# First dilated attention: dilated units and cross-attention units in alternation

## The reference, cut to what matters

```python
for g, (window, dilation) in enumerate(((128, 1), (512, 4), (2048, 16))):      # 4 heads of 128 each
    o, lse = dilated_window_attention(q[:, :, sl], k[:, :, sl], v[:, :, sl], window, dilation)
# softmax over the three groups' lse weighs their outputs; 512 columns come out

p = softmax(einsum('bshd,bmhd->bhsm', q, k) * XA_HEAD_DIM ** -0.5)             # 4 heads of 64, 256 memory tokens
o = einsum('bhsm,bmhd->bshd', p, v)                                            # 256 columns, beside the 512
```

## Time and profile before

| | us |
|---|---|
| median of 3 runs (lowest to highest) | 2457.7 (2454.57 to 2458.89) |
| the profiled execution, as timed | 2457.92 |
| its span, first to last instruction | 2456.1 |
| in it, `da0`, from its first weight load on PE to its last output copy | 1315.97 to 1379.38 |

### The profile page before, as it was taken

How to read it: one execution, slowest core, us unless ns; L and a number is a source line. 1 busy time by engine, 2 the same in 40 slices (tenths; PEclk the granted TensorE clock), 3 DMA queues, 4 the chain that set the end, 5 groups by cost and what they waited for, 6 DMA issues and landing times. The chain is left out here.

```text
span 2456.1 us, 32385 instructions
## 1 busy us (share of the span) xinstructions
PE 2395.0 (98%) x11700; PEld 2030.8 (83%) x11700; DVE 1722.0 (70%) x2910; ACT 1030.7 (42%) x2126; POOL 200.8 (8%) x269
## 2 busy tenths in 40 slices
PE   7999999999999999999999999999999999999998
PEld 7998877888888888878888889887788888888877
DVE  4522564479899989896653563563679998998996
ACT  6433553344444444446334433433344444443443
POOL 2010012000000000003212021121100000000000
PEclk9999999999999999999999999999999999999999
DMA  4230122222222248743102111212632222227863
GB/s 148 83 104 20 40 84 61 86 72 84 79 94 86 77 139 305 268 133 129 52 18 83 35 35 45 60 35 75 210 96 78 86 78 78 95 81 258 292 191 126
DMA packets 206517, 257.72 MB, mean 105 GB/s; under 512 B 38376, under 2 KB 141784, under 8 KB 206360
## 3 DMA queue, kind: packets, MB, share of 16 engines
q1 hardware_dynamic: 202200, 255.65, 31.7%
q10 hardware_dynamic: 4160, 0.02, 0.1%
HBM read 206.54 MB, written 49.09 MB: 104 GB/s over the span
## 5 line engine op out<-in xcount | busy, mean ns | idle before, releaser
L52 PE MATMUL psum<-f_T_lo 128*128 128x512 f32 x616 | 241.6, 392 | 1.4 <-DVE f_T_lo L683 0.8
L53 PE MATMUL psum<-f_T_lo 128*128 128x512 f32 x616 | 239.8, 389 | 0.0
L54 PE MATMUL psum<-f_T_lo 128*128 128x512 f32 x616 | 239.8, 389 | 0.0
L52 PE MATMUL psum<-w_hi,hT_hi 128*128 128x512 f32 x576 | 229.3, 398 | 3.9 <-DVE w_lo L1469 2.2
L54 PE MATMUL psum<-w_hi,hT_lo 128*128 128x512 f32 x576 | 226.4, 393 | 0.0
L53 PE MATMUL psum<-w_lo,hT_hi 128*128 128x512 f32 x576 | 226.1, 393 | 0.0
L52 PEld LDWEIGHTS psum<-w_hi,hT_hi 128*128 128x128 f32 x576 | 124.8, 217 | 22.0 <-issue 3.6
L52 PEld LDWEIGHTS psum<-f_T_lo 128*128 128x128 f32 x616 | 115.6, 188 | 30.5 <-DVE f_T_lo L683 7.1
L54 PEld LDWEIGHTS psum<-w_hi,hT_lo 128*128 128x128 f32 x576 | 125.0, 217 | 18.0
L53 PEld LDWEIGHTS psum<-w_lo,hT_hi 128*128 128x128 f32 x576 | 125.1, 217 | 16.7
L52 PE MATMUL psum<-hT_hi,f_up_hi 128*128 128x512 f32 x352 | 137.4, 390 | 0.4 <-DVE f_up_lo L622 0.4
(11 more groups left out here) (434 smaller groups left out, 6014.6 us busy)
## 6 DMA issues: line engine op xcount, KB each, us to landing
raw<-in_ffn_w_up_dram SPq DMA_DIRECT2D x88, 512.0 KB, 4.7
activations<-f_act SPq DMA_DIRECT2D x44, 512.0 KB, 2.6
w_raw<-in_b_w_in_dram SPq DMA_DIRECT2D x18, 1024.0 KB, 6.2
f_up_pieces<-activations SPq DMA_DIRECT2D x30, 512.0 KB, 4.4
f_up_pieces<-in_ffn_w_down_dram SPq DMA_DIRECT2D x22, 512.0 KB, 4.9
x_between<-XY SPq DMA_DIRECT2D x16, 512.0 KB, 5.1
XY<-x_between SPq DMA_DIRECT2D x16, 512.0 KB, 6.6
w_raw<-in_a_w_in_dram SPq DMA_DIRECT2D x8, 768.0 KB, 5.8
```

The costliest lines, as they stand in the source:

```text
L52: nc.tensor.matmul(out, lhs_hi, rhs_hi, start=start, stop=False)
L53: nc.tensor.matmul(out, lhs_hi, rhs_lo, start=False, stop=False)
L54: return nc.tensor.matmul(out, lhs_lo, rhs_hi, start=False, stop=stop)
```

## The change

The list of `da0` is put in another order. The first two staged tiles (8 units) stay in front. Behind them, 24 pairs follow, each of one staged unit and one cross unit, until the staged units are used up; the last 8 cross units end the list. Each unit gets a kind, "staged" or "rest", and a number among those of its kind. What was found by a unit's place in the list (the column of its row sum, its tile in the store's count, the wait for the loaded keys) is found by kind and number. SP waits for the place of a tile's fourth head before it stores the tile, and for that of the last staged unit before it stores the row sums.

```diff
+    kinds = [u[7] for u in units]
+    number = [kinds[0:i].count(kinds[i]) for i in range(U)]
+    place = [i for i in range(U) if kinds[i] == "staged"]
+    first_rest = kinds.index("rest") if "rest" in kinds else U
...
         def neg_top(u):
-            return group_top[:, u:u + 1] if u < staged else rest_top[:, u - staged:u - staged + 1]
+            return (group_top if kinds[u] == "staged" else rest_top)[:, number[u]:number[u] + 1]
...
-                    if loads and i == staged:
+                    if loads and i == first_rest:
                         pe.wait_ge(loaded, 16 * len(loads))
...
-                    if u >= staged:
+                    if kinds[u] == "rest":
                         nc.vector.reciprocal(total(u), total(u)).then_inc(inverted, 1)
...
-                    if u < staged:
-                        if u % 4 == 0 and stage.before(u // 4):
-                            act.wait_ge(stage.stored[u // 4 % 2], stage.before(u // 4))
+                    if kinds[u] == "staged":
+                        t = number[u] // 4
+                        if number[u] % 4 == 0 and stage.before(t):
+                            act.wait_ge(stage.stored[t % 2], stage.before(t))
                         nc.scalar.activation(out, src, ACT.Copy).then_inc(out_done, 1)
                     else:
-                        act.wait_ge(inverted, u - staged + 1)
+                        act.wait_ge(inverted, number[u] + 1)
...
             for t in range(TT):
-                sp.wait_ge(out_done, 4 * t + 4)
+                sp.wait_ge(out_done, place[4 * t + 3] + 1)
                 stage.store(sp, t)
...
             if U > staged:
-                sp.wait_ge(expd, staged)
+                sp.wait_ge(expd, place[-1] + 1)
                 stage.store_sums(sp)
...
-                        units += xa_units(lambda h, t: XQ[:, t, h // 2 * P:(h // 2 + 1) * P], keys, vals, D_DIL)
+                        cross = xa_units(lambda h, t: XQ[:, t, h // 2 * P:(h // 2 + 1) * P], keys, vals, D_DIL)
+
+                        both = [u for pair in zip(units[2 * DIL_HEADS:], cross) for u in pair]
+                        units = units[0:2 * DIL_HEADS] + both + cross[len(both) // 2:]
```

## The result

The changed kernel takes 2461.93 us in the median (20 runs, 2457.1 to 2464.57), the kernel before in runs beside it 2458.52 (20 runs, 2453.3 to 2462.76). The ratio is 1.0014, with a 95% interval of 1.0008 to 1.0020: 3.4 us slower, a small loss that is real. 2461.9 was forecast.

The account below looks back on a forecast made before the run. PE, busy 98% of the span, was taken as the bound, so only its waits and clock in `da0` could change. Pairs 41.58, cross steps, end and low clock made 54.3 us against 50.31: 2457.92 + 4.0 = 2461.9, range 2456 to 2466.

Parts of the forecast that it names:

- The pair: In da0's alternation, one staged plus one cross step would take 1.98 us against 1.755 before, 0.225 lost on each.
- the last piece: End of the cross units' loop on PE, product's weight load to next scores: 0.39 us, or 0.45 with PE full.
- The chain: Cross units' two-step loop through PE and DVE: scores, reduction, copy, product, next cross scores; 1.95 to 2.01 us.
- The waits named beforehand: PE's weight load of the cross product would wait about 0.3 us for DVE's copy, 20-odd times; staged products no more.
- The hole: PE's idle stretch early in da0, while ACT waits for staging tile 0's store; would shrink from 3.7 to about 2.4 us.
- low piece: Stretch of about 3.4 us behind PE's idle stretch in da0 with PE at half clock, costing 1.36 us after the change.
- the third rival: PE's clock stays up after the shorter idle stretch in da0: 1.36 us comes off, +2.6, 2460.5 us; chance 0.17.
- The sum: From unit 14's scores to da0's end: 54.3 us after against 50.31 before, a difference of +4.0 us.
- PE alone: Rival: PE's own work sets each staged-and-cross pair in da0 at 1.66 us; -2.7, 2455.2 us; chance 0.08.
- the plain sum: Rival: a staged-and-cross pair in da0 costs its parts, 1.755 us; -0.7, 2457.2 us; chance 0.07.
- The clock in the alternation: Rival: PE's clock falls during da0's pairs, half of 41.6 us at 1.2 GHz; +8 more, 2470 us; chance 0.06.
- DVE's order: Rival: in da0 a late staged copy delays the cross reduction by up to 0.29 us a pair; 2468 us; chance 0.06.

Follow-up runs that it names:

- the lengthened loop: Changed kernel plus a second DVE copy of 128 columns of each cross unit's transposed probabilities, ahead of the real copy: 2467.48 us, one run.

## Why the prediction was right

**The pair.** This was the step that carried the forecast, and it held: 2.01 us where 1.95 to 2.01 was given and 1.98 taken. Of the two values for the last piece, product to next scores, 0.39 and 0.45, the second was the right one. The 0.39 came from the drain, where transposes follow and not scores. That is 0.03 x 21 = 0.6 us too little. The chain was shown from three sides: the rows after, a copy added to it (+0.19 a pair with DVE idle), and one step more of distance (1.66).

**The waits named beforehand** are there: 28 waits of a product for its copy. 24 are of cross units: 20 in the pairs behind the hole with 0.33 us each, and four of 0.22 to 0.42 ahead of the hole, at the last pair and at the end. The other 4 are of staged units ahead of the hole, and no staged product waits in the pairs behind it.

**The hole.** The scores of unit 14 started 13.27 us into the phase, 0.17 later than before. PE had 1.2 us more work behind it when its wait began, where 1.1 to 1.4 was given, and with the later end the wait shrank from 3.74 to 2.68 and not to 2.4. That it only shrinks and doesn't go was right. ACT's wait for the store went from 3.89 to 3.27, so it shrank by 0.6 where about 1.3 was named; it is PE's wait that the sum needs.

**The clock.** The forecast kept one low piece behind the hole at 1.36 us. In the profile after there was none, which was the third rival. The second profile of the kernel before had none either, and the lengthened loop had one behind a shorter hole, 2.5 us. So the low piece can't be counted on for either kernel. The step that failed is that I kept it on both sides, with 1.21 in the sum of before and 1.36 in that of after, and gave its absence a chance of only 0.17. The two nearly cancel, so that without either the forecast would have been +3.85 and not +4.0. That it cost so little is luck.

**The sum.** From the scores of unit 14, 54.3 us were forecast and 53.4 measured (41.85 for the 21 pairs, 7.54 for the 7 cross steps, 3.98 to the end). The terms: pairs 41.58 taken, 41.85 measured, since the first pair behind the hole took only 1.69; low clock 1.36 taken, 0 measured; the rest within 0.2. Against the first profile of the kernel before (50.31, low piece and all) the measured sum gives +3.1, and +3.2 with the later end of the hole; against the second (49.69) it gives +3.7, and +4.3 without that one's second wait. The forecast's +4.0 stands among these; the medians give +3.4, with an interval of 2 to 5. So the record bears out the mechanism, and the size to within a us. That the median of the time came out at the forecast 2461.9 itself is luck: the kernel before had a median of 2458.52 beside it, 0.6 more than the 2457.92 that the forecast was counted from, and that makes up for what the change cost less than +4.0.

**The rivals.** PE alone (1.66) and the plain sum (1.755) are excluded by the 19 pairs at 2.01. The clock in the alternation stayed at 1.00 with PE busy for 36.48 of 38.16 us by its records. DVE's order added nothing: the cross reduction began as soon as its scores were there. The page "Perfetto Trace Analysis" (Optimization Strategy) of the Trainium skill says that interleaving regimes may help where the most-contended engine changes over time. In this kernel it depended on how: in ones, with the distance as it was, the interleaved regimes took 2.01 us a pair and the separate ones 1.755; with the product a step later a pair took 1.66; and four cross units in one piece, put where PE stood idle, brought the time to 2451.03 from 2457.93.

## What to carry to other kernels

In a pipeline written out by step, look for the loops that come back to the same engine after k steps. In steady state each runs through units at a distance of k, so alternating two kinds with k = 2 gives the slow kind a loop of its own. Where that loop is longer than the busiest engine's own work for the pair, as 2.01 was here against 1.66, each pair pays the difference, and idle time on the engines doesn't help. Compare the loop's length with the engine's work in the same k steps before reordering; its slack can be read as the difference between the end of a copy and the start of what needed it. A hole with one cause and one place wants a block of work at that place, as large as the hole, and not a new order for the whole phase. Here taking the cause away, by issuing two loads later, did much the same (ratio 0.9980 for it, 0.9972 for the block).

## What the runs showed of the hardware that I had not expected

The length of the hole doesn't tell whether the clock falls behind it: at 3.74 us of idle PE it fell (0.61 from 1328.8 to 1333.0), at 2.80, 2.77 and 2.68 it stayed up, and at 2.50 it fell (0.54 from 1329.5 to 1333.0). Each is one profile, and the kernels differ, so what decides it is open.

`da0` started anywhere from 1312.9 to 1317.5 us in the twelve profiles taken since the first, with nothing changed ahead of it. The starts go with where the granted clock had been low before: three profiles, the first among them, ran at half clock for a piece each at 251, 323, 388 and 1162 us and start `da0` at 1315.9; four with such pieces at 320, 385 and 1160 alone start it at 1312.9 to 1313.2. That alone is 3 us, a good part of the 4 to 9 us between runs of one kernel. Differences of 3 us need twenty runs, or a phase cut out of the profile and read step by step.
